# A transformer block pair on one core: another order of transfers, conversions and groups where the gated stages turn from their up to their down products

## The reference, cut to what matters

```python
# first stage ("f1"), in first_block
x_new = x_new + g2 * ((silu(h2 @ w_gate) * (h2 @ w_up)) @ w_down)

# second stage ("f2"), in second_block
u = causal_dwconv(h @ w_up, conv_w, conv_b)      # 3 taps along the tokens
g, val = split(u, 2, axis=-1)
x = x + (silu(g) * val) @ w_down
```

## Time and profile before

| what | value |
|---|---|
| median of 3 runs | 2770.87 us (2764.04 to 2771.69) |
| profiled execution | 2767.5 us |
| span of its trace | 2765.7 us |
| PE matmuls busy | 2611.5 us (94%) |
| VectorE busy | 1470.7 us (53%) |
| ScalarE busy | 1051.2 us (38%) |
| GpSimd busy | 1144.0 us (41%) |
| mean granted TensorE clock | 0.977 of full speed |

### The profile page before, as it was taken

The page is one execution under the profiler, slowest core; times in us unless marked ns, Lnnn a source line. Parts: engine busy times, 40 slices in busy tenths (PEclk is TensorE's granted clock), DMA queues, the critical chain, the costliest instruction groups (busy, mean ns, idle before and its releaser), DMA issues.

```text
span 2765.7 us, 33008 instructions
## 1 busy us (share of the span) xinstructions
PE 2611.5 (94%) x12564; PEld 2101.4 (76%) x12564; DVE 1470.7 (53%) x1910; ACT 1051.2 (38%) x1706; POOL 1144.0 (41%) x690
## 2 busy tenths in 40 slices
PE   7999999999789999998999999999988999997997
PEld 5787679889668888887886677667867888876885
DVE  5552279989338656555332311124178788765333
ACT  5523457877434233331113341224235444431113
POOL 0212322463356555555444311113464555555354
PEclk9999999999999999999999999999999999998998
DMA  7441020221321222226233011001411222234321
GB/s 276 137 161 53 22 58 17 52 74 50 119 94 54 77 92 78 76 69 209 90 98 105 31 38 39 23 24 34 151 59 56 82 92 84 84 111 145 110 77 61
DMA packets 70300, 232.49 MB, mean 84 GB/s; under 512 B 8305, under 2 KB 10481, under 8 KB 70018
## 3 DMA queue, kind: packets, MB, share of 16 engines
q1 hardware_dynamic: 70146, 230.39, 25.2%
HBM read 179.77 MB, written 39.85 MB: 79 GB/s over the span
## 4 chain that ended last, share of the span: by engine, by line
PE 84%; DVE 7%; ACT 3%; issue 3%; POOL 1%; DMA 1%; SPq 0%; DVEq 0%; ACTq 0%; POOLq 0%
PE S L812 17%; PE S L451 12%; PE S L452 11%; PE S L791 9%; PE S L795 9%; PE S L792 9%; PE S L667 3%; PE M L683 2%; PE M L895 1%; PE S L760 1%; PE S L651 1%; PE M L454 1%; PE S L652 1%; PE S L910 1%; PE S L614 1%
## 5 line engine op out<-in xcount | busy, mean ns | idle before, releaser
L2067 POOL TENSOR_TENSOR wbl<-rf,wbh 128x512 fp32r<-128x512 f32 (+1 forms) x352 | 508.1, 1449 | 525.0 <-ACT wbh L1175 524.6
L1175 ACT ACTIVATE wbh<-rf 128x512 fp32r<-128x512 f32 (+1 forms) x352 | 215.6, 620 | 719.6 <-PE S L812 380.0
L1953 POOL TENSOR_TENSOR wl<-raw,wh 128x1024 fp32r<-128x1024 f32 x59 | 142.9, 2423 | 630.6 <-ACT wh L964 630.6
L791 PE MATMUL S<-th_t,wbh 128*128 128x512 f32 x640 | 251.4, 393 | 2.6 <-POOL wbl L2067 2.6
L795 PE MATMUL S<-tl_t,wbh 128*128 128x512 f32 x640 | 250.9, 392 | 0.0
L792 PE MATMUL S<-th_t,wbl 128*128 128x512 f32 x640 | 250.3, 391 | 0.0
L812 PE MATMUL S<-fh,wbh 128*128 128x512 f32 x704 | 220.9, 395 | 26.9 <-DVE xt L1651 18.3
L451 PE MATMUL S<-hh,wh 128*128 128x512 f32 (+1 forms) x472 | 203.6, 431 | 25.1 <-ACT hh L1157 6.6
L812 PE MATMUL S<-fh,wbl 128*128 128x512 f32 x704 | 219.7, 393 | 0.0
L812 PE MATMUL S<-fl,wbh 128*128 128x512 f32 x704 | 219.2, 393 | 0.0
L1651 DVE TENSOR_TENSOR xt<-S,xt 128x1024 f32<-128x1024 f32 (+1 forms) x58 | 68.5, 1186 | 238.0 <-PE S L812 160.0
(11 more groups left out here) (325 smaller groups left out, 5789.0 us busy)
## 6 DMA issues: line engine op xcount, KB each, us to landing
ff<-hid SPq DMA_DIRECT2D x44, 512.0 KB, 6.1
rf<-in_w_d SPq DMA_DIRECT2D x80, 256.0 KB, 2.7
mr<-in_w_modT SPq DMA_DIRECT2D x32, 512.0 KB, 4.6
rf<-in_w_f1g SPq DMA_DIRECT2D x22, 512.0 KB, 3.6
rf<-in_w_f1u SPq DMA_DIRECT2D x22, 512.0 KB, 3.4
hid<-pr SPq DMA_DIRECT2D x22, 512.0 KB, 2.7
rf<-in_w_f2g SPq DMA_DIRECT2D x22, 512.0 KB, 5.2
rf<-in_w_f2u SPq DMA_DIRECT2D x22, 512.0 KB, 3.6
```

The costliest lines, as they stand in the source:

```text
L791: e.matmul(o, hi[:, k, :], th[part][:, k, :], start=k == 0, stop=False)
L1175: e.activation(flat(wbh[wslot(f, n)][:, :, :])[:, 0:x.shape[1]], x, ACT.Copy).then_inc(*w_hi.mark((f, n)))
L1953: e.tensor_tensor(l, raw[:, w % 3, 0:n], h.bitcast(F), ALU.subtract).then_inc(*w_lo.mark(w))
L2067: e.tensor_tensor(l, x, h.bitcast(F), ALU.subtract).then_inc(*w_lo.mark((f, n)))
```

## The change

The change alters the order of work where each of the two stages turns from up to down; the work itself stays.

- Groups: `DNG` becomes [4, 2, 4, 4, 4, 4], so group 0 has four hidden blocks and group 1 two. PE takes PSUM buffers 2 and 0 for its first two output blocks and not 0 and 1 (`SL.i = 2`).
- DVE and POOL: hidden blocks 0 and 1 are converted where they were (after product `NP-3`); 2 and 3 right after product `NP-1`; 4 to 7 each behind one of group 0's first four output blocks. In f2, DVE's taps of the last pair come behind the conversion of 2 and 3.
- ACT and POOL: the weight blocks `NP+4` and `NP+5` are rounded behind the whole up part (behind the last taps) and not within it.
- SP: the weights of blocks `NP+4` and `NP+5` are loaded between `load_hidden` 3 and 4. `xt` is read back as its place comes free: in f1 `xt[0..3]` during pairs 8 to 11, for which `sg` moves by 16 KB; in f2 `xt[0]` and `xt[1]` between `load_hidden` 5 and 6, and the others between and behind the last stores. `load_x` gets the waits that this needs.

```diff
-DNG = [2, 4, 4, 4, 4, 4]
+DNG = [4, 2, 4, 4, 4, 4]
...
-    sg = at("sg", U, [128, 2, 1024], F)
+    sg = at("sg", U + 16 * KB, [128, 2, 1024], F)
...
-                SL.i = 0
+                SL.i = 2
...
-                block_hi(f, w0, t + RING)
+                if t < NP - 2:
+                    block_hi(f, w0, t + RING)
...
                 for t in range(NF, NP):
                     after(f, w0, t)
+                block_hi(f, w0, NP + 4)
+                block_hi(f, w0, NP + 5)
...
-                if p == 4:
+                if p == 4 and q < NPAIR - 1:
                     taps(q, 0)
                     taps(q, 1)
...
-                    if t == NP - 3:
+                    if t in (NP - 3, NP - 1):
                         for a in range(2):
-                            hidden(f, dn, a)
+                            hidden(f, dn, a + t - NP + 3)
+                    if f == "f2" and t == NP - 1:
+                        taps(NPAIR - 1, 0)
+                        taps(NPAIR - 1, 1)
...
-                    if g == 0 and m == 0:
-                        for a in range(2, 8):
-                            hidden(f, dn, a)
-                        e.wait_ge(*l_xt((8 if f == "f1" else 24) + m))
-                    elif g == 0:
+                    if g == 0:
                         e.wait_ge(*l_xt((8 if f == "f1" else 24) + m))
                     residual(m, (f, t), (f, t), None if gate is None else gate[:, m:m + 1], last and m == 7)
+                    if g == 0 and m < 4:
+                        hidden(f, dn, 4 + m)
...
+                    if f == "f1" and 8 <= q < 12:
+                        load_x(f, q - 8)
...
                     load_hidden(f, a)
-                for r in range(NSLAB + 4, NSLAB + 9):
+                    if a == 3:
+                        load_rf(f, NSLAB + 4)
+                        load_rf(f, NSLAB + 5)
+                    if f == "f2" and a == 5:
+                        load_x(f, 0)
+                        load_x(f, 1)
+                for r in range(NSLAB + 6, NSLAB + 9):
                     load_rf(f, r)
-                store_hidden(f, last)
-                for k in range(6):
-                    load_x(f, k)
+                if f == "f2":
+                    load_x(f, 2)
+                    store_hidden(f, last, (0,))
+                    load_x(f, 3)
+                    load_x(f, 4)
+                    store_hidden(f, last, (1,))
+                else:
+                    store_hidden(f, last)
+                    load_x(f, 4)
+                load_x(f, 5)
                 load_rf(f, NSLAB + 9)
...
```

More of the change, by code:

```diff
@@ L2100, in ffn @@
                 for t in range(NF, NP):
-                    block_lo(f, t + RING)
-                    if t == NP - 3:
+                    if t < NP - 2:
+                        block_lo(f, t + RING)
+                    if t in (NP - 3, NP - 1):
                         for a in range(2):
-                            hidden(dn, a)
+                            hidden(dn, a + t - NP + 3)
+                block_lo(f, NP + 4)
+                block_lo(f, NP + 5)
                 for g, m in DOWN:
-                    if g == 0 and m == 0:
-                        for a in range(2, 8):
-                            hidden(dn, a)
                     block_lo(f, down_at(g, m) + RING)
+                    if g == 0 and m < 4:
+                        hidden(dn, 4 + m)
                     if g == len(DNG) - 1:
@@ L2274, in keep_x, with store_hidden @@
                 e.dma_start(T["keep" + f[1]][k], xt[:, k, :]).then_inc(*l_keep.inc(k + (8 if f == "f2" else 0)))
-            def store_hidden(f, q):
-                for s in range(2):
+            def store_hidden(f, q, parts=(0, 1)):
+                for s in parts:
                     a = 2 * (q // 2) + s
@@ L2291, in load_x @@
             def load_x(f, k):
+                last = NPAIR - 1
+                if f == "f1":
+                    if k < 4:
+                        e.wait_ge(*p_tl((f, "b22", 3)))
+                        e.wait_ge(*d_t((f, "t4", 3)))
+                    elif k < 6:
+                        e.wait_ge(*d_mul((f, last, 21)))
+                    else:
+                        e.wait_ge(*l_hid(NHID - 2 + k - 6))
+                elif k < 4:
+                    e.wait_ge(*d_tap((f, last - 1 + k // 2, k % 2, 1)))
+                elif k < 6:
+                    e.wait_ge(*d_mul((f, last, k - 4)))
+                    e.wait_ge(*d_tap((f, last, 1, 1)))
+                else:
+                    e.wait_ge(*l_hid(2 * NHID - 2 + k - 6))
+                    e.wait_ge(*d_mul((f, last, 1)))
                 e.wait_ge(*l_keep(k + (8 if f == "f2" else 0)))
@@ L2320, in ffn @@
                     load_hidden(f, a)
-                for r in range(NSLAB + 4, NSLAB + 9):
-                    load_rf(f, r)
-                store_hidden(f, last)
-                for k in range(6):
-                    load_x(f, k)
-                load_rf(f, NSLAB + 9)
[L2327 to L2331, removed]
+                    if a == 3:
[5 more added lines that the diff above has]
+                for r in range(NSLAB + 6, NSLAB + 9):
+                    load_rf(f, r)
+                if f == "f2":
[4 more added lines that the diff above has]
+                    store_hidden(f, last, (1,))
+                else:
+                    store_hidden(f, last)
+                    load_x(f, 4)
+                load_x(f, 5)
+                load_rf(f, NSLAB + 9)
+                load_x(f, 6)
+                load_x(f, 7)
                 for n in range(10, len(DOWN)):
```

## The result

| | before | changed |
|---|---|---|
| median | 2771.28 us (2764.04 to 2772.04, 4 runs) | 2742.53 us (2739.43 to 2744.56, 4 runs) |
| span of the profiled execution | 2765.7 us | 2740.5 us |

The ratio is 0.990, with a 95% interval of 0.9886 to 0.9914. The change is faster by 28.7 us by the medians and by 25.2 us by the profiled spans. 2746 us was predicted, 2737 to 2757 as the range.

What follows compares the result with a forecast made beforehand. PE is busy nearly throughout, so only its idle time and the slow clock behind it can be won. Gains of 8.5 (f1) and 14.5 us (f2) sum to 23.0, from 2767.5 to 2744.5, or 2747.9 from the median; 2746 taken, range 2737 to 2757.

Steps and rivals of the forecast that it cites:

- What each turn lost: Turns from up to down: 10.3 us in f1 and 21.8 in f2 beyond matmul time, together a ceiling of 32.1 us.
- f1, 8.5 us forecast: Turn of f1: of 10.3 us lost, 1.8 stays as waits for POOL's subtractions 1 and 2, so 8.5 is gained.
- the x move: Earlier reads of x: claimed no help in f1 in any case, as the roundings bound the first addition there.
- f2, 14.5 us forecast: Turn of f2: of 21.8 us lost, 7.3 stays (waits 1.2 and 4.0, slow clock 2.1), so 14.5 is gained.
- times alone, added: DVE and POOL at f2's turn: their times alone add to 19.6 us from 2479.24, so DVE is through at 2498.8.
- The wait for subtraction 3: PE in f2: needs it at 2487.6, there at 2488.6, as a tap gets in between; waits 1.2 us in all.
- DVE and POOL take turns: Roundings, taps, products and POOL's work share an exclusive lock: a rounding of 0.69 us alone takes 2.83 beside POOL.
- The rival of no turns: DVE's work at f2's turn runs beside POOL's: no wait before the fourth output block, 2737 to 2740 us; chance 0.2.
- Groups 1 and 2, the rival of the other side: Boundary of groups 1 and 2: PE waits for subtraction 8 or a weight block, kernel slower, 2784 us; chance 0.02.
- The ACT order: ACT before f2's taps: stood 10.03 us for weight block NP+4's load, so the taps started only at 2485.17.
- The base: Start of the sum: profiled execution 2767.5 us gives 2744.5; the median 2770.87, 3.4 above it, gives 2747.9.

Runs made afterwards that it cites:

- e9: Changed kernel with e6's edit, and in f1 DVE making hidden block 2's low part between its roundings of 2 and 3: turns 66.1 and 66.6 us, median 2738.63 us.
- e1: Changed kernel with all reads of x back behind the last stores: turns 71.6 (f1) and 77.4 us (f2), median 2752.83 us.
- e7: Changed kernel with DVE, not POOL, making the low parts of hidden blocks 2 and 3 in f2: f2 turn 67.8 us, median 2738.50 us.
- e3: Changed kernel with DVE's last taps of f2 ahead of the roundings of hidden blocks 2 and 3: f2 turn 75.1 us, median 2747.86 us.
- e6: Changed kernel with f2's first residual addition between the taps of the last pair's two halves: f2 turn 66.6 us, median 2739.53 us.
- e5: Kernel before, with only ACT rounding weight blocks NP+4 and NP+5 behind the last taps: turns 76.5 and 83.5 us, median 2765.79 us.
- e2: Changed kernel with ACT rounding weight blocks NP+4 and NP+5 ahead of the taps again: turns 67.3 and 71.1 us, median 2742.86 us.
- e10: Changed kernel with PE taking PSUM buffers 0 and 1 first again (SL.i = 0): turns 68.4 and 69.7 us, median 2742.78 us.

## Why the prediction was right, and where it was not

**What each turn lost.** Right: 10.3 and 21.8 us above the matmuls' own time were the ceiling. Against e9's 66.1, the shortest turn, it is 10.0 and 21.5. The spans differ by 25.2 us and the two turns by 25.3.

**f1, 8.5 us forecast, 8.8 measured.** The waits were at POOL's subtraction, as said, 0.96 us and not 1.8; subtraction 1 was in time. One sentence was wrong as a statement on the parts: that the x move "is none in any case" in f1. By the rows it was no help in the old order, where the first addition followed the roundings without a gap, but it is what the new order stands on: e1 costs 4.3 us in f1. The step that was wrong is the reading of SP's list. I had named that SP stands before weight load 8 until POOL has done block `NP+4`, but had costed it only for x[2] and later in f2, not for x[0] in f1 if that had stayed behind it. It made no error in the sum, as the change does move x.

**f2, 14.5 us forecast, 16.5 measured.** The mechanism was right: the same wait, shorter, at the fourth output block, DVE through its list before it, and a slow clock behind it. Three sizes were off:
- DVE ended its list 18.6 us into the down part, not 20.4. After the end of subtraction 1 (2472.5) the times alone add to 17.6 us (two roundings, two subtractions, four taps, two products, three weight blocks), and it took 15.7. So "times alone, added" came out 1.9 us too long. Much of that is that rows overlap a little: the roundings end at 2471.10 + 2.53 = 2473.63 in the list above, and the first tap starts at 2473.55; 13 such steps of some 0.1 us are 1.3 by estimate. The rest is open.
- The wait for subtraction 3 was 0.27 us and not most of 1.2.
- The wait came to 2.60 and not 4.0, and the clock to 1.8 and not 2.1. Sum 4.7 where I had 7.3, 2.6 less, of which 2.0 shows in the gain: the turn before had lost 21.5 us and not 21.8, and the changed one is 5.0 us above e9's 66.1, 0.3 more than the sum.

**DVE and POOL take turns.** Right, shown by e7: less shared time and more DVE time gave an earlier addition. The Trainium skill's rule of the exclusive lock (SBUF — State Buffer, "SBUF: two separate sides") holds here: two taps took 6.76 us beside two subtractions of 2.4 each, and 2.59 us without them. One conclusion that the prediction drew from it was wrong: that it speaks against putting conversions 2 and 3 ahead of the taps. e3 turns the order round and loses 4.0 us, since PE needs hidden block 2 first. The rival of no turns (2737 to 2740) is out, though its time was nearly met: what it would have needed, no wait before the fourth block, is what e6 makes.

**Groups 1 and 2, the rival of the other side.** No wait of PE stands there in the changed kernel; its only waits for a down part's operands are the three shown.

**The ACT order.** The text took the wait of 10.03 us as the cause of the late taps, and e5 shows it (4.1 us). What it did not see is that the new place of the loads and DVE's new order cure it without ACT's (e2).

**The base.** 25.2 us by the profiled executions lies 2.2 above the sum of 23.0. The rest of the 28.7 us by the medians is where the profiled execution of before lay in its runs, 3.8 below their median.

## What to carry to other kernels

Look for the one instruction whose operands are long there and which stands in its engine's list behind work for later: here a residual addition of 1.2 us behind taps or roundings held PE for 2.6 to 18 us, and moving that one instruction (e6) gained 4.5 us, more than the 3.3 us of DVE taking over POOL's two subtractions (e7). Before costing two engines side by side, see whether a row of the one grows beside the other; if so, add their times; here that sum was 1.9 us above the measured 15.7. And test each part of a change from both sides: ACT's order was worth 4.1 us alone and 0 in company, the x reads were worth nothing in the old order of f1, by its rows, and 4.3 us in the new one (e1).

## What the runs showed of the hardware

The granted clock after a short idle stretch of PE is not a matter of its length alone. Behind 1.90 us in e10's f2 it fell to the lower level and cost 1.7 us; behind 2.25 us in e10's f1 it did not fall, nor behind 2.63 us early in f2 of the kernel before. Behind 2.39 us in e1's f1 and 2.60 us in the changed kernel's f2 it fell, and cost 1.9 and 1.8; behind 4.63 us it cost 2.1. What a removed wait of 2 to 3 us is worth is thus, in these runs, itself plus 0 or about 2 us.

The two that did not slow the clock, e10's f1 and the kernel before:

```profile
1263.72 0.71 PE L813 MATMUL S<-fh,wbh 128*128 128x512 f32 x2 [2.25 <-DVE pr L1753]
1264.26 0.62 PE L813 MATMUL S<-fh,wbl 128*128 128x512 f32 x2
```

```profile
2101.67 0.47 PE L791 MATMUL S<-th_t,wbh 128*128 128x512 f32 x1 [2.63 <-POOL wbl L2067]
2101.97 0.40 PE L792 MATMUL S<-th_t,wbl 128*128 128x512 f32 x1
```
